# GpSimd takes low parts at the entry of an expert stage, and the unsplit half loads move from few-token to many-token steps

## The chip, the core and the metric

The kernel runs on one core of a Trainium2 chip. The metric is the device time of one execution in microseconds. Engines: TensorE (PE; its weight loads are PEld), VectorE (DVE), ScalarE (ACT), GpSimd (POOL), and SyncE (SP), which issues the loads from HBM.

## What is computed

Two layers of an encoder trunk over 256 tokens of width 1024, all in float32. The first layer ends in a dense feed-forward, the second in a mixture of eight experts, two chosen for each token. The expert part of the reference, cut to its core:

```python
logits = (t @ router)
top_v, top_i = lax.top_k(logits, 2)
top_w = jax.nn.softmax(top_v, axis=-1)
gates = sum(one_hot(top_i, 8) * top_w[..., None], axis=1)
for e in range(8):
    out = out + gates[:, e:e + 1] * ((silu(t @ w1[e]) * (t @ w3[e])) @ w2[e])
```

w1 and w3 are 1024 x 3584, w2 is 3584 x 1024. The change touches nothing ahead of this part but the routing.

## The kernel before, in words

**Split products.** A float32 product is made from faster fp32r matmuls: each operand is split into a high part (the value rounded to fp32r) and a low part (value minus high part), and three products are summed: high x high, low x high, high x low. ScalarE makes the high part of a weight (w_hi, L648), VectorE the low part (w_lo, L654). The unit of this is the half: half of a 1 MB load, 128 x 1024 elements. The program has 672 halves in the expert stage. Buffers for six split halves exist (AHEAD): ScalarE may make the high part of a half when TensorE has used the one six before.

**Experts and steps.** An expert's 3584 hidden columns are worked in 7 steps of 512, so there are 56 steps. A step has 12 halves: four of w1 (h1), four of w3 (h3), four of w2. The experts are put in an order by their number of tokens, known only at run time: positions 1, 3, 5, 7 (SMALL) have at most 64 tokens, the others at most 128. "(3,2)" is step 2 of position 3. Few-token and many-token steps alternate, after two many-token ones. TensorE's order in step i is: h1 of i, the turning of the hidden rows of step i-1 (with a fold, L1223, if that was a few-token step, or transposes, L1225), h3 of i, then w2 of step i-1. So w2 comes one step late: a few-token step's h1 and h3 are followed by the w2 of a many-token step.

**Two kinds of halves.** In a many-token step, tokens' high and low parts are two stationary operands: six matmuls of 512 columns for a half (L1154, L1155, L1158). In a few-token step the high parts of 64 tokens and their low parts share one stationary operand of 128 columns, so a half takes four (L1107, L1110), and the two sets of rows are added afterwards.

**Unsplit halves.** In some few-token steps (those of number 0, 2, 4, 6, so 16 in all) the third half of h1 isn't split: TensorE multiplies the raw float32 weights with unsplit tokens (h_few, its columns from 64 up set to zero once) in two float32 matmuls, each shown as two records (L1119). ScalarE and VectorE leave these halves out. The load's slot in the ring of ten is then free only when TensorE has used the half, while a split half frees it as soon as its low part is made.

**Order of VectorE's work in the stage.** It goes through the halves u in order; for each it does what hangs on it and then splits the half six split halves on (next_lo). At the first half of h3 of step i it makes the low part of the hidden rows of step i-1 (lower: L2211 for a many-token step, L2208 for a few-token one), which w2 of step i-1 waits for. At the second it forms other operands, at the last the product with silu (L2239). Tokens of the next expert are brought in at its eve (gather, or turn_rows at L1198), the picks of the expert after (choose, L2108) are made in step 3, its slots are told (L1213) in step 4.

**Entry.** ScalarE makes the first six high parts while VectorE computes the top two. VectorE makes the low part of half 0, then the chain of small operations: places, the picks of the first expert (choose(0)), the counts' order, most_i (the largest count, on which all engines branch between this path and a general one), then the permutation of the experts (perm_i, which SyncE reads before it can load the second expert, from the 11th load on), then the places arranged by it. After the branch it makes the low parts of the first tokens and of halves 1 to 5. TensorE gathers the first expert's tokens, with unneeded matmuls ahead (keep_busy) that keep it from falling idle. GpSimd has nothing to do there. SyncE's 11th load waits for the low parts of halves 0 and 1.

Of the kernel before, what the change touches and what calls it, by code (L numbers as in the profile page):

```python
# [14 lines left out]
P = 128  # L15
# [17 lines left out]
E = 8  # L33
# [12 lines left out]
AHEAD = 6  # L46
SMALL = (1, 3, 5, 7)
# [4 lines left out]
WHOLE_STEPS = (0, 2, 4, 6)  # L52
LAST_Q = 3
FEW_K = 2 * WHOLE_Q - 4
# [151 lines left out]
def is_few(i):  # L206
    return SEQ[i][0] in SMALL
# [7 lines left out]
class Experts:  # L215


    def __init__(self):
        self.loads = []
        for i in range(STEPS + 1):  # L220
            if i < STEPS:
                self.loads += [("h1", i, 0), ("h1", i, 1), ("h3", i, 0), ("h3", i, 1)]
            if i >= 1:
                self.loads += [("w2", i - 1, 0), ("w2", i - 1, 1)]
        self.first = {key: 2 * n for n, key in enumerate(self.loads)}
        self.halves = 2 * len(self.loads)
        self.whole = {self.first[("h1", i, 0)] + WHOLE_Q for i in range(STEPS) if is_few(i) and SEQ[i][1] in WHOLE_STEPS}
        self.split = [m for m in range(self.halves) if m not in self.whole]
        self.rank = {m: r for r, m in enumerate(self.split)}
# [7 lines left out]
def trunk_kernel(nc, x, norm1_g, w_in, w_gate, b_gate, w_branch, w_out, pool_w, pool_scale,  # L237
# [7 lines left out]
    with ExitStack() as ctx:  # L245
# [134 lines left out]
        h_few = mix(2, P)  # L380
# [59 lines left out]
        half_lo_done = sem("half_lo_done")  # L440
        half_used = sem("half_used")
# [90 lines left out]
        h_few_zero = sem("h_few_zero")  # L532
# [101 lines left out]
        def wait_half_lo(eng, m):  # L634

            eng.wait_ge(half_lo_done, m + 1)
# [14 lines left out]
        def split_half_lo(eng, m, r, halves=1):  # L651
# [4 lines left out]
                .then_inc(half_lo_done, halves)  # L656
# [94 lines left out]
        def _(pool):  # L751
# [37 lines left out]
            for l in range(L):  # L789
                pool.affine_select(out=ws[:, l, :, :], in_=ws[:, l, :, :], compare_op=ALU.is_ge, fill=0.0, base=0,  # L790
                                   pattern=[[0, 4], [-1, P]], channel_multiplier=1).then_inc(ws_lower, 1)

# [27 lines left out]
        def _(pe):  # L820
# [276 lines left out]
            keep_busy(6)  # L1097
# [30 lines left out]
            def inner_few(kind, i, toks, b, gathers=None):  # L1128
                for q in range(4):
# [3 lines left out]
                    if m in ex.whole:  # L1133
                        half_whole(m, [(h_few[:, k, :], slice(MU * k, MU * k + MU), bank[b][:, :]) for k in range(2)])
                        continue
                    outs = [(h_hi[:, 2 * q + k, toks], slice(MU * k, MU * k + MU), bank[b][:, :]) for k in range(2)]
                    half_few(m, outs, lambda x: q == 0 and x == 0, lambda x: q == LAST_Q and x == 1)
# [23 lines left out]
            def inner(kind, i, tiles, rank, gathers=None):  # L1161

                for q in range(4):
# [4 lines left out]
                    m = ex.first[(kind, i, 0)] + q  # L1168
                    half(m, rank(m), outs, lambda x: q == 0 and x % 2 == 0, lambda x: q == 3 and x % 2 == 1)
# [170 lines left out]
        def _(act_e):  # L1340
# [245 lines left out]
            def gathered_hi(e, c, b):  # L1586
                act_e.wait_ge(gathered, 2 * e + c + 1)
                n = FEW if e in SMALL else CAP
                if e in SMALL and c == 1:
                    act_e.wait_ge(h_few_zero, 1)  # L1590
                    fn(h_few[:, :, 0:FEW], bank[b][:, :].rearrange("p (k n) -> p k n", k=4)[:, FEW_K:FEW_K + 2, 0:FEW], ACT.Copy)
# [99 lines left out]
        def _(dve):  # L1691
# [438 lines left out]
            dve.tensor_reduce(most[:, :], counts[:, 0:E], AX, ALU.max)  # L2130
            step(tt(more, down(cnt), across(cnt), ALU.is_gt))
            step(dve.tensor_reduce(order, more, AX, ALU.add))
            step(ts(last_small, order, len(SMALL) - 1.0, None, ALU.is_equal))
            step(tt(last_small, last_small, counts[:, 0:E], ALU.mult))
            step(dve.tensor_reduce(third[:, :], last_small, AX, ALU.add))
            ts(most_i[:, :], third[:, :], CAP / FEW, most[:, 0:1], ALU.mult, ALU.max).then_inc(most_ready, 1)

# [31 lines left out]
            arrange(0, place, place_p)  # L2169
            dve.wait_ge(sent, 2)  # L2170
# [42 lines left out]
            def gathered_experts():  # L2213
                gathered_lo(0, 0, 5)
                split_half_lo(dve, 1, 1)
                gathered_lo(0, 1, 7)
                for m in range(2, AHEAD):
                    split_half_lo(dve, m, m)
                choose(1)
                dve.memset(h_few[:, :, FEW:P], 0.0).then_inc(h_few_zero, 1)  # L2220
# [41 lines left out]
            def all_tokens():  # L2262
# [5 lines left out]
                for m in range(1, AHEAD):  # L2268
                    split_half_lo(dve, m, m)
# [90 lines left out]
```

## Time and profile before

| | us |
|---|---|
| median of 3 runs | 1502.58 (1502.07 to 1504.14) |
| the profiled execution | 1503.12 |
| its span, first to last instruction | 1501.4 |
| TensorE busy / VectorE / ScalarE | 1452.4 / 1262.9 / 1096.6 |
| expert stage, first to last expert matmul | 626.7 to about 1491 |

The granted clock of TensorE is 0.993 of full speed over the span. From about 595 us on, the DMA engines are busy nearly without a break, at 405 to 423 GB/s in most slices. In the windows of rows 3, the stretches are the steps (1,0), (0,2), (1,1), (3,1) and (7,2). To read the rows below: times are from the span's start, and matmuls are pipelined, so a group's start to the next group's start is what it costs, not its busy time.

### The profile page before, as it was taken

The page shows a single profiled execution, that of the slowest core. Times are in us where ns is not written, and L with a number is a line of the kernel's source. Part 1 is how long each engine was busy: PE and PEld are TensorE (multiplying, and loading weights), DVE is VectorE, ACT ScalarE, POOL GpSimd, SP SyncE. Part 2 cuts the span into 40 slices and gives each one's busy share as a digit, 9 for nine tenths or more (in the row PEclk, how much of TensorE's full clock was granted, in tenths as well). Part 3 has the DMA queues.
Part 4 walks back from the last instruction along what each step waited for, and adds up shares of the span by engine and source line. Part 5 has one row for each costly group of instructions (what it writes and reads, how often), then busy time and mean ns, then how long its engine had stood idle before and what let it go on. Part 6 is the DMA issues. An engine that isn't in the chain of part 4 may idle for free.

```text
span 1501.4 us, 22229 instructions
## 1 busy us (share of the span) xinstructions
PE 1452.4 (97%) x8407; PEld 1259.6 (84%) x8407; DVE 1262.9 (84%) x1408; ACT 1096.6 (73%) x1306; POOL 94.6 (6%) x48
## 2 busy tenths in 40 slices
PE   7999989999999999999999999999999999999996
PEld 7999969999899998888877877787877887778884
DVE  5887775454588867799999999999999999999996
ACT  5685553333457663678888888888898889898885
POOL 4000000000000000000000031000040000040001
PEclk9999999999999999999999999999999999999998
DMA  9545336555444443999999999999999999999993
GB/s 278 200 148 193 141 142 222 177 188 193 144 169 173 177 158 132 408 359 421 409 421 409 409 405 416 420 421 405 412 413 423 420 409 408 421 416 421 421 421 117
DMA packets 66439, 467.02 MB, mean 311 GB/s; under 512 B 7658, under 2 KB 7894, under 8 KB 11030
## 3 DMA queue, kind: packets, MB, share of 16 engines
q1 hardware_dynamic: 63878, 458.27, 76.2%
q0 software_dynamic: 2400, 7.24, 2.4%
q8 instruction: 69, 1.13, 0.3%
q14 instruction: 44, 0.36, 0.1%
q10 hardware_dynamic: 48, 0.02, 0.0%
HBM read 460.26 MB, written 5.24 MB: 310 GB/s over the span
## 4 chain that ended last, share of the span: by engine, by line
PE 71%; DVE 19%; ACT 6%; issue 2%; DMA 1%; POOL 0%; DVEq 0%; SPq 0%; ACTq 0%
DVE w_lo L654 13%; PE bank L844 9%; PE bank L845 9%; PE bank L846 9%; PE bank L1154 9%; PE bank L1158 9%; PE bank L1155 9%; PE bank L1110 4%; PE bank L1107 4%; PE bank L1119 1%; ACT w_hi L582 1%; DMA ring<-in_w_in 1%; PE bank L1223 1%; ACT w_hi L648 1%; DVE w_lo L590 1%
## 5 line engine op out<-in xcount | busy, mean ns | idle before, releaser
L654 DVE TENSOR_TENSOR w_lo<-arena,w_hi 128x1024 fp32r<-128x1024 f32 x528 | 617.6, 1216 | 28.4 <-ACT w_hi L648 24.4
L648 ACT ACTIVATE w_hi<-arena 128x1024 fp32r<-128x1024 f32 x528 | 533.7, 1053 | 60.2 <-PE bank L1158 56.7
L590 DVE TENSOR_TENSOR w_lo<-ring,w_hi 128x2048 fp32r<-128x2048 f32 x94 | 214.9, 2289 | 128.2 <-ACT w_hi L582 127.1
L844 PE MATMUL bank<-h_hi,w_hi 128*128 128x256 f32 x992 | 283.2, 285 | 1.8 <-DVE h_lo L1748 1.7
L845 PE MATMUL bank<-h_lo,w_hi 128*128 128x256 f32 x992 | 280.6, 283 | 0.0
L846 PE MATMUL bank<-h_hi,w_lo 128*128 128x256 f32 x992 | 280.6, 283 | 0.0
L582 ACT ACTIVATE w_hi<-ring 128x2048 fp32r<-128x2048 f32 x94 | 179.7, 1913 | 105.5 <-PE bank L846 80.0
L844 PEld LDWEIGHTS bank<-h_hi,w_hi 128*128 128x128 f32 x992 | 190.2, 192 | 4.0 <-issue 2.9
L845 PEld LDWEIGHTS bank<-h_lo,w_hi 128*128 128x128 f32 x992 | 190.3, 192 | 0.5
L846 PEld LDWEIGHTS bank<-h_hi,w_lo 128*128 128x128 f32 x992 | 190.2, 192 | 0.0
L1154 PE MATMUL bank<-w_hi,h_hi 128*128 128x512 f32 x448 | 177.3, 396 | 0.0
L1155 PE MATMUL bank<-w_hi,h_lo 128*128 128x512 f32 x448 | 174.6, 390 | 0.0
L654 DVE TENSOR_TENSOR w_lo<-ring,w_hi 128x1024 fp32r<-128x1024 f32 x128 | 150.9, 1216 | 4.4 <-ACT w_hi L648 3.8
L648 ACT ACTIVATE w_hi<-ring 128x1024 fp32r<-128x1024 f32 x128 | 130.5, 1053 | 12.9 <-PE bank L1158 12.4
L1158 PE MATMUL bank<-w_lo,h_hi 128*128 128x512 f32 x448 | 138.3, 390 | 0.3 <-DVE w_lo L654 0.3
L1107 PE MATMUL bank<-w_hi,h_hi 128*128 128x512 f32 x416 | 137.5, 412 | 0.0
L1110 PE MATMUL bank<-w_lo,h_hi 128*128 128x512 f32 x416 | 128.9, 391 | 0.0
L1158 PEld LDWEIGHTS bank<-w_lo,h_hi 128*128 128x128 f32 x448 | 84.0, 188 | 18.9 <-DVE w_lo L654 0.8
L1154 PE MATMUL bank<-w_hi,act_hi 128*128 128x512 f32 x224 | 90.1, 402 | 8.8 <-DVE act_lo L2211 8.6
L1154 PEld LDWEIGHTS bank<-w_hi,h_hi 128*128 128x128 f32 x448 | 84.2, 188 | 16.8
L1155 PEld LDWEIGHTS bank<-w_hi,h_lo 128*128 128x128 f32 x448 | 84.2, 188 | 16.6
L1107 PEld LDWEIGHTS bank<-w_hi,h_hi 128*128 128x128 f32 x416 | 76.1, 188 | 20.5 <-issue 7.7
(308 smaller groups left out, 2189.9 us busy)
## 6 DMA issues: line engine op xcount, KB each, us to landing
arena<-in_moe_w SPq DMA_DIRECT2D x270, 1024.0 KB, 10.7
ring<-in_moe_w SPq DMA_DIRECT2D x66, 1024.0 KB, 10.7
ring<-in_ffn_w SPq DMA_DIRECT2D x33, 1024.0 KB, 4.8
ring<-in_w_gate SPq DMA_DIRECT2D x32, 1024.0 KB, 4.8
ring<-in_w_in SPq DMA_DIRECT2D x15, 1024.0 KB, 6.4
ring<-in_w_branch SPq DMA_DIRECT2D x8, 1024.0 KB, 4.7
ring<-in_w_out SPq DMA_DIRECT2D x8, 1024.0 KB, 4.8
x_tok<-in_x SPq DMA_DIRECT2D x2, 512.0 KB, 4.2
```

What stands on the lines that cost most here:

```text
L582: nc.scalar.activation(w_hi[:, m % HI, :], raw, ACT.Copy).then_inc(hi_ready[m % HI], 1)
L590: nc.vector.tensor_tensor(w_lo[:, m % LO, :], raw, w_hi[:, m % HI, :].bitcast(F32), ALU.subtract)\
L648: nc.scalar.activation(half_hi[:, r % AHEAD, :], raw_of(n)[:, HALF * (m % 2):HALF * (m % 2) + HALF], ACT.Copy)\
L654: eng.tensor_tensor(half_lo[:, r % AHEAD, :], raw_of(m // 2)[:, HALF * (m % 2):HALF * (m % 2) + HALF], half_hi[:, r % AHEAD, :].bitcast(F3 ...
L844: pe.matmul(out_, a[0], b[0], start=start, stop=False)
L845: pe.matmul(out_, a[0], b[1], start=False, stop=False)
L846: return pe.matmul(out_, a[1], b[0], start=False, stop=stop)
L1107: pe.matmul(dst, both, w[:, cols], start=first(x), stop=False)
L1110: last = pe.matmul(dst, both, wl[:, cols], start=False, stop=final(x))
L1154: pe.matmul(dst, hi, w[:, cols], start=first(x), stop=False)
L1155: pe.matmul(dst, lo, w[:, cols], start=False, stop=False)
L1158: last = pe.matmul(dst, hi, wl[:, cols], start=False, stop=final(x))
```

## The change

Four things are done.

1. The unsplit halves: none in few-token steps now; the third half of h1 in every many-token step but the first of all, 27 in all. The stationary operand h_whole holds all 128 tokens, and is written by ScalarE when it takes a many-token expert's tokens.
2. The low parts of halves 1, 2 and 3 are made by GpSimd, with a semaphore of their own. VectorE makes those of halves 4 and 5 after the branch.
3. VectorE computes the order and perm_i first and most_i after them; the places are arranged behind the branch, between the low parts of the tokens.
4. Four unneeded matmuls ahead of the first gather instead of six; the zeroing of h_few goes.

```diff
+POOL_LO = (1, 2, 3)
-WHOLE_STEPS = (0, 2, 4, 6)
-        self.whole = {self.first[("h1", i, 0)] + WHOLE_Q for i in range(STEPS) if is_few(i) and SEQ[i][1] in WHOLE_STEPS}
+        self.whole = {self.first[("h1", i, 0)] + WHOLE_Q for i in range(1, STEPS) if not is_few(i)}
...
         def wait_half_lo(eng, m):
-            eng.wait_ge(half_lo_done, m + 1)
+            if m in POOL_LO:
+                eng.wait_ge(pool_lo_done, POOL_LO.index(m) + 1)
+            else:
+                eng.wait_ge(half_lo_done, m + 1)
...
+            for m in POOL_LO:
+                split_half_lo(pool, m, m)
...
-            keep_busy(6)
+            keep_busy(4)
...
             def inner_few(kind, i, toks, b, gathers=None):
-                    if m in ex.whole:
-                        half_whole(m, [(h_few[:, k, :], slice(MU * k, MU * k + MU), bank[b][:, :]) for k in range(2)])
-                        continue
...
             def inner(kind, i, tiles, rank, gathers=None):
+                    if rank(m) is None:
+                        half_whole(m, [(h_whole[:, k, :], slice(MU * k, MU * k + MU), bank[tiles[0][1]][:, :]) for k in range(2)])
+                        continue
...
             def gathered_hi(e, c, b):
-                if e in SMALL and c == 1:
-                    act_e.wait_ge(h_few_zero, 1)
-                    fn(h_few[:, :, 0:FEW], bank[b][:, :].rearrange("p (k n) -> p k n", k=4)[:, FEW_K:FEW_K + 2, 0:FEW], ACT.Copy)
+                if e not in SMALL and c == 1:
+                    fn(h_whole, bank[b][:, :].rearrange("p (k n) -> p k n", k=4)[:, WHOLE_K:WHOLE_K + 2, :], ACT.Copy)
...
             step(tt(cnt, tie, counts[:, 0:E], ALU.add))
-            dve.tensor_reduce(most[:, :], counts[:, 0:E], AX, ALU.max)
             step(tt(more, down(cnt), across(cnt), ALU.is_gt))
             step(dve.tensor_reduce(order, more, AX, ALU.add))
-            step(ts(last_small, order, len(SMALL) - 1.0, None, ALU.is_equal))
-            step(tt(last_small, last_small, counts[:, 0:E], ALU.mult))
-            step(dve.tensor_reduce(third[:, :], last_small, AX, ALU.add))
-            ts(most_i[:, :], third[:, :], CAP / FEW, most[:, 0:1], ALU.mult, ALU.max).then_inc(most_ready, 1)
...
             dve.tensor_copy(perm_i[:, :], perm).then_inc(perm_ready, 1)
-            arrange(0, place, place_p)
-            dve.wait_ge(sent, 2)
+            dve.tensor_reduce(most[:, :], counts[:, 0:E], AX, ALU.max)
+            step(ts(last_small, order, len(SMALL) - 1.0, None, ALU.is_equal))
+            step(tt(last_small, last_small, counts[:, 0:E], ALU.mult))
+            step(dve.tensor_reduce(third[:, :], last_small, AX, ALU.add))
+            ts(most_i[:, :], third[:, :], CAP / FEW, most[:, 0:1], ALU.mult, ALU.max).then_inc(most_ready, 1)
...
             def gathered_experts():
                 gathered_lo(0, 0, 5)
-                split_half_lo(dve, 1, 1)
+                arrange(0, place, place_p)
                 gathered_lo(0, 1, 7)
-                for m in range(2, AHEAD):
-                    split_half_lo(dve, m, m)
+                for m in range(4, AHEAD):
+                    split_half_lo(dve, m, m, 1 if m > 4 else 1 + len(POOL_LO))
+                dve.wait_ge(sent, 2)
                 choose(1)
-                dve.memset(h_few[:, :, FEW:P], 0.0).then_inc(h_few_zero, 1)
```

## Rows read from the trace of the kernel before

**Rows 1.** The page, part 1: busy us (share of the span) xinstructions.
```profile
PE 1452.4 (97%) x8407; PEld 1259.6 (84%) x8407; DVE 1262.9 (84%) x1408; ACT 1096.6 (73%) x1306; POOL 94.6 (6%) x48
```

**Rows 2.** The page's costliest groups: busy us, mean ns, idle before.
```profile
L654 DVE TENSOR_TENSOR w_lo<-arena,w_hi 128x1024 fp32r<-128x1024 f32 x528 | 617.6, 1216 | 28.4 <-ACT w_hi L648 24.4
L648 ACT ACTIVATE w_hi<-arena 128x1024 fp32r<-128x1024 f32 x528 | 533.7, 1053 | 60.2 <-PE bank L1158 56.7
```

**Rows 3.** Windows: length; busy PE, PEld, DVE, ACT, POOL; PEclk, DMA share, GB/s.
```profile
658.90:673.15 14.25, 14.25 (x62) 11.09 (x61) 12.33 (x13) 12.53 (x15) 0.00 (x0) 1.00 0.81 329
673.15:688.60 15.45, 15.45 (x73) 12.91 (x72) 15.07 (x15) 12.99 (x15) 0.00 (x0) 1.00 1.01 424
688.60:703.20 14.60, 13.63 (x62) 10.95 (x61) 14.60 (x15) 14.26 (x17) 0.00 (x0) 1.00 1.01 418
...
905.77:920.82 15.05, 13.67 (x63) 10.95 (x61) 15.05 (x15) 14.38 (x17) 0.00 (x0) 1.00 1.02 406
...
1366.30:1380.60 14.30, 14.30 (x62) 11.11 (x62) 13.56 (x14) 12.98 (x16) 0.00 (x0) 1.00 1.01 421
```

**Rows 4.** The chain that ended last, 1340 to 1482: start, us, what.
```profile
1356.51 0.84 PE bank L1223 x8
...
1386.23 0.84 PE bank L1223 x8
...
1394.26 10.21 DVE w_lo L654 x9
1404.47 0.61 DVE act_lo L2211
...
1416.31 0.84 PE bank L1223 x8
```

**Rows 5.** Waits from 660 to 1480, SyncE's from 600: total us, times, longest.
```profile
PE bank L1154 <- DVE act_lo L2211: 8.6, 9, 1.4
...
ACT w_hi L648 <- PE bank L1158: 61.7, 201, 2.3
...
SPq L745 <- PE bank L1119: 54.7, 15, 5.1
```

**Rows 6.** Timeline of TensorE in (1,2) and (0,3): start, us, what, count.
```profile
719.64 0.62 PE L1107 MATMUL bank<-w_hi,h_hi 128*128 128x512 f32 x2
...
720.55 0.62 PE L1107 MATMUL bank<-w_hi,h_hi 128*128 128x512 f32 x2
...
724.11 0.60 PE L1225 MATMUL bank<-const,qk_raw 128*128 128x128 f32 x4
...
703.24 0.39 PE L1154 MATMUL bank<-w_hi,h_hi 128*128 128x512 f32 x1
...
704.60 0.39 PE L1154 MATMUL bank<-w_hi,h_hi 128*128 128x512 f32 x1
```

**Rows 7.** Timeline: the telling in (1,4), the picks, VectorE in (3,0).
```profile
788.38 0.50 PE L1213 MATMUL bank<-of_token,arena 128*128 128x2 f32 x4
...
722.00 0.47 DVE L2108 TENSOR_SCALAR arena<-const,place_p 128x128 f32<-128x128 f32 x2
...
878.90 2.36 DVE L654 TENSOR_TENSOR w_lo<-arena,w_hi 128x1024 fp32r<-128x1024 f32 x2 [1.99 <-ACT w_hi L648]
```

**Rows 8.** Entry: timeline, chain, one window, SyncE's issues, GpSimd's select early on.
```profile
612.94 5.77 ACT L648 ACTIVATE w_hi<-arena 128x1024 fp32r<-128x1024 f32 x6
...
626.65 0.50 PE L1154 MATMUL bank<-w_hi,h_hi 128*128 128x512 f32 x1
...
635.18 1.14 DVE w_lo L654
...
615.50:626.60 11.10, 11.06 (x56) 9.37 (x55) 8.08 (x39) 5.30 (x7) 0.00 (x0) 0.69 1.01 414
...
628.77 18.76 SPq L745 DMA_DIRECT2D arena<-in_moe_w  x8
...
L790 POOL TENSOR_SCALAR_AFFINE_SELECT arena<-arena 128x512 f32<-128x512 f32 x2 | 3.8, 1927 | 8.2 <-DMA arena<-in_sgu_w 8.2
```

More of the change, by code:

```diff
@@ L51 @@
 WHOLE_Q = 2
-WHOLE_STEPS = (0, 2, 4, 6)
-LAST_Q = 3
-FEW_K = 2 * WHOLE_Q - 4
+WHOLE_K = 2 * WHOLE_Q - 4
 MORE = 8
@@ L379, in trunk_kernel @@
         picks = mix(2, TT, CAP)
-        h_few = mix(2, P)
+        h_whole = mix(2, P)
         half_hi = w_hi[:, :, :].rearrange("p a (b c) -> p (a b) c", c=HALF)
@@ L440, in trunk_kernel @@
         half_lo_done = sem("half_lo_done")
+        pool_lo_done = sem("pool_lo_done")
         half_used = sem("half_used")
@@ L531, in trunk_kernel @@
         eye_set = sem("eye_set")
-        h_few_zero = sem("h_few_zero")
         gate_ready = sem("gate_ready")
@@ L655, in split_half_lo @@
                               half_hi[:, r % AHEAD, :].bitcast(F32), ALU.subtract)\
-                .then_inc(half_lo_done, halves)
+                .then_inc(pool_lo_done if m in POOL_LO else half_lo_done, halves)
         def drams(key):
@@ L1132, in inner_few @@
                     m = ex.first[(kind, i, 0)] + q
-                    if m in ex.whole:
-                        half_whole(m, [(h_few[:, k, :], slice(MU * k, MU * k + MU), bank[b][:, :]) for k in range(2)])
-                        continue
                     outs = [(h_hi[:, 2 * q + k, toks], slice(MU * k, MU * k + MU), bank[b][:, :]) for k in range(2)]
-                    half_few(m, outs, lambda x: q == 0 and x == 0, lambda x: q == LAST_Q and x == 1)
+                    half_few(m, outs, lambda x: q == 0 and x == 0, lambda x: q == 3 and x == 1)
                     if kind == "h3" and q == 0:
@@ L2267, in all_tokens @@
                         .then_inc(all_lo, 1)
-                for m in range(1, AHEAD):
-                    split_half_lo(dve, m, m)
+                for m in range(4, AHEAD):
+                    split_half_lo(dve, m, m, 1 if m > 4 else 1 + len(POOL_LO))
+                arrange(0, place, place_p)
+                dve.wait_ge(sent, 2)
                 weights()
```

## Prediction

> **What bounds the kernel now.** I read the page first. TensorE is busy for 1452 us of the span and VectorE for 1263 us [rows 1], so the shares alone say that TensorE is the limit, with VectorE next. The change works almost wholly in the expert stage, from about 626 us to 1490 us. I read that stage from three views.
>
> First the engine times of single steps [rows 3], each from its first h1 matmul to the next step's. A many-token step takes 15.45 us and TensorE is busy for all of it, while VectorE is busy for 15.07. A few-token step with an unsplit half takes 14.30 us, all of it TensorE, with VectorE at 13.56. A few-token step without one takes 14.60 us, but there VectorE is busy for all of it and TensorE for only 13.63. So the bound alternates: TensorE in many-token steps, VectorE in few-token steps that have all their halves split.
>
> Then the chain of waits [rows 4], whose fold of hidden rows (L1223, once in each many-token step) marks pairs of steps. The pair from 1356.51 to 1386.23 has an unsplit half and takes 29.72 us. The pair from 1386.23 to 1416.31 has none and takes 30.08 us; its chain passes through act_lo at L2211. The pair with more TensorE work is the shorter one.
>
> Last the waits [rows 5]: in the expert stage TensorE waits for L2211 and ScalarE for TensorE; no compute engine waits for a transfer there. Why L2211 is late in a few-token step: twelve "fast" halves lie in a row (w2 of the step before last, then h1 and h3 of this one), each 0.91 us on TensorE against 1.13 us on VectorE (1.216 us long, but nine in 10.21 us as they overlap) [rows 2, 4, 6]. VectorE works at most six halves ahead, and L2211 waits in its order behind the splits. In the "slow" stretch (w2 of a many-token step, h1, h3, at 1.36 us a half [rows 6]) VectorE catches up, and idles: 0.38 us of step 673.15 to 688.60 [rows 3].
>
> **The change part by part.** The profiled execution took 1503.12 us (span 1501.4); the median of the runs shown is 1502.58, 0.5 us less. Sums are made against 1503.12.
>
> *Price of an unsplit half on TensorE.* In few-token step (1,2) the four halves of h1 run from 719.64 to 724.11, 4.47 us; the first takes 0.91 (719.64 to 720.55). So the unsplit one costs 4.47 - 3 x 0.91 = 1.74 us, its slow successor included [rows 6]. In a few-token step it replaced four matmuls: +0.83. In a many-token step it replaces six, 1.36 us (703.24 to 704.60): +0.38, and I use 0.37 from the mean of all.
>
> *A. 27 unsplit halves added in many-token steps (steps 1 to 55).* TensorE bounds these steps, and their VectorE and ScalarE have idle time already. The unsplit half lies at h1, the third of its step. The split it spares VectorE falls six halves earlier, in the slow stretch, where VectorE catches up anyway; five split halves more follow before the fast stretch, so VectorE enters that with the same full lead as before. Nothing is given back: 27 x 0.37 = **+10.0 us**.
>
> *B. 16 unsplit halves taken out of few-token steps.* TensorE does 0.83 us less, VectorE one split more (1.13), in the middle of the fast stretch. The step turns into the VectorE-bound kind that the trace shows: the pair goes from 29.72 to 30.08, +0.36 [rows 4]. So taken for the five later steps with nothing else in them ((1,6), (3,6), (5,6), (7,2), (7,4)): +1.8. In (1,4), (3,4), (5,4) the matmuls that tell the slots (0.50 us long, some 0.36 of it by itself, L1213) lie ahead of w2 and hide that much [rows 7]: 0. In (1,2), (3,2), (5,2) VectorE also makes the picks (0.47 us, 0.4 with the overlap, L2108 [rows 7]): about +0.75 each; in the first of them two tellings give TensorE 0.9 us of other work, so only +0.15: together +1.65. Sum **+3.4**.
>
> *C. First steps of the few-token experts.* In (3,0) ScalarE first empties the results and VectorE then stands idle for 1.99 us waiting for it [rows 7]; one more high part there (1.05 us, [rows 2]) goes straight in front of ScalarE's next work, which TensorE's join waits for: +1.0, three times ((3,0), (5,0), (7,0)). In (1,0) VectorE is busy for only 12.33 of 14.25 us [rows 3], so it loses 0.83 and gets back some 0.3 of stall: -0.5. Sum **+2.5**.
>
> *D. Second steps (3,1), (5,1), (7,1).* VectorE comes into them behind, from the step before; the unsplit half in the many-token step between lets it catch up. They fall from the 15.05 us that (3,1) takes [rows 3] to the 14.60 of (1,1): three times 0.4, **-1.2**.
>
> *E. Entry.* GpSimd takes the low parts of halves 1 to 3, that is 3 x 1.13 = 3.4 us from VectorE; the rearranging of the places (0.6 us) moves behind the branch. The six high parts are made from 612.94 to 618.7, one each 0.96 us, and TensorE starts half 0 at 626.65 [rows 8], so it wants the low part of half 1 at about 628 and of half 3 at 631. GpSimd's speed is not in the trace: at VectorE's pace 1.2 us a half, by its nearest row (a select over 128x512, 1.93 us [rows 8]) 3.9 us, which ends the third at about 615 + 11.6 = 626.6. Both are in time, so the speed costs nothing. The only stall that VectorE's backlog makes here is at the low part made from 635.18 to 636.32, 0.6 us on TensorE (half 6 takes 1.97 us in place of 1.36) [rows 8]: gone. most_i comes some 0.9 us later (behind the four steps of the order), and TensorE's first expert matmul follows ScalarE's and VectorE's branch: the gather's end is no longer what counts, so two keep-busy matmuls less buy nothing: 626.65 to about 626.9, +0.2. The order's earlier end lets SyncE issue the eleventh load about 4 us sooner (628.77 before); behind it wait all later loads, and no engine waits for loads. Sum -0.4, and +0.3 for port sharing (below): **-0.1**. The Trainium skill ("GPSIMD Engine Reference", 3.1 Elementwise) puts a two-input operation of 2048 columns at 4497 ns on GpSimd and 2293 on VectorE; the trace's 1216 ns for 1024 columns on VectorE fits that [rows 2], GpSimd's isn't shown. By it, an estimate from that page, a half takes 2.4 us and the sum stays as it is.
>
> *F. End.* Step (7,6) is the last, and behind it only the last splits are made, ScalarE's and then VectorE's. It loses its unsplit half: -0.83 if TensorE set the end, +1.13 if the last low part does [rows 2]. The trace's chain ends on ScalarE and VectorE there, with some idle time ahead of them: **+0.4**.
>
> Total 10.0 + 3.4 + 2.5 - 1.2 - 0.1 + 0.4 = +15.0, or 1518.1 against the profiled run, 1517.6 as a median.
>
> **The rivals.**
> *R1, faster: the spared splits are shared.* 27 instead of 16 halves unsplit takes 11 x 1.13 = 12.4 us off VectorE. If VectorE's lead at the start of the fast stretch grew with the many-token step's unsplit half, the few-token steps would lose their stall as well. Then TensorE's sum decides: +10.0 - 16 x 0.83 - 0.7 = -4.0, **1498.6**. For it: VectorE is full in those steps. Against: it idles just before them, so its lead is capped by buffers, not by work. It decides if no TensorE wait for L2211 is left in a common few-token step; from an average stall of 0.5 instead of 1.2 us in 28 steps the time is still near 1507.
> *R2, slower still: GpSimd disturbs the routing at the entry.* Its operations run from 615 to 619 at the least and 626.6 at the most, beside VectorE's chain of small ones, which is on the path: VectorE is busy for 8.08 us from 615.50 to 626.60 [rows 8], of which 1.22 and 0.69 are larger ones with slack. If the 6.2 left took twice as long, the time would be 1517.6 + 6.2 - 0.3 = **1523.5**. The trace has no such overlap; the chain's operations are tiny, which speaks against the full price, so I carry 0.3. The Trainium skill says in the same page (1. Specifications) that GpSimd shares its SBUF interfaces with VectorE instructions that have two SBUF inputs; most of the chain's have. That speaks for this rival.
> *R3: the ring of loads.* SyncE can refill a slot whose half is unsplit only when TensorE has used it; such waits are 54.7 us in 15 now [rows 5] and become 27. In 658.90 to 673.15 the DMA share fell to 0.81; in 1366.30 to 1380.60, also with such a wait, it stayed 1.01 [rows 3]: the queue is deep enough later. If it drained each time, 0.2 x 14 = 2.8 us of transfer would be lost in each pair, and beyond a few pairs the loads would set the pace: about **1530** at 10 pairs. Slower steps make it less likely.
> *R4: the change doesn't do what it says.* A stall partly relieved and an unsplit half somewhat dearer behind other matmuls: within 1509 to 1513.
>
> **How the numbers follow.** Forecast 0.77, **1517.6** (own range 1513 to 1522, from B between 0 and +6 and the entry); R1 0.08; R2 0.08; R3 0.02; R4 0.05. The range 1509 to 1523.5 leaves out R1, R3 and the far end of R2. A measurement tells 0.2% (3 us) from no change: faster is 0.07, same 0.04 (the space between R1 and R4), slower 0.89.
>
> **What would show it.** A: each many-token step 15.8 instead of 15.45 us with TensorE busy throughout, and 108 fp32 matmul records instead of 64. B: pairs of about 30.45 us, act_lo (L2211 of before) on the chain in nearly every one, and TensorE's wait for it up from 8.6 us in 9 to some 20 in 25. C, D: (3,0) at 17.1, (3,1) at 14.6. E: the wait at 635 gone, the eleventh load issued near 624.5. The forecast is wrong if few-token steps come out at 13.5 us (R1), if the stretch from 615 to 627 grows by over a microsecond (R2), or if ScalarE or TensorE waits for a load (R3).

## Result and the profile after

The changed kernel's median is 1527.05 us (1523.68 to 1529.20, five runs), against 1502.58 before (1502.07 to 1504.14, also five). The ratio is 1.0163, 95% interval 1.0148 to 1.0178: slower by 24.5 us. The forecast was 1517.6 with a range to 1523.5: the direction was right, the size 9.4 us short and outside the range. The profiled execution took 1524.43 us (span 1522.7), 21.3 more than the profiled one of before.

The page's busy line and its two costliest groups, which answer [rows 1, 2]:

```profile
PE 1453.9 (95%) x8351; PEld 1251.2 (82%) x8351; DVE 1250.7 (82%) x1393; ACT 1083.4 (71%) x1295; POOL 99.7 (7%) x51
...
L656 DVE TENSOR_TENSOR w_lo<-arena,w_hi 128x1024 fp32r<-128x1024 f32 x515 | 600.8, 1216 | 49.9 <-ACT w_hi L650 46.7
L650 ACT ACTIVATE w_hi<-arena 128x1024 fp32r<-128x1024 f32 x518 | 522.7, 1053 | 55.8 <-PE bank L1160 52.4
```

VectorE has 12 us less work and TensorE 1.5 more, and the kernel is 21 longer: nearly all of it went into waits of TensorE. The windows of the steps (1,0), (0,2), (1,1), (3,0), (3,1) and (7,2), with the columns of [rows 3]:

```profile
665.51:679.07 13.56, 13.56 (x63) 11.01 (x62) 13.40 (x14) 13.40 (x16) 0.00 (x0) 1.00 0.98 360
679.07:694.89 15.82, 15.82 (x72) 12.55 (x71) 14.01 (x14) 11.92 (x14) 0.00 (x0) 1.00 0.94 388
694.89:709.53 14.64, 13.67 (x63) 10.95 (x62) 14.64 (x15) 14.13 (x17) 0.00 (x0) 1.00 1.00 412
883.69:900.58 16.89, 14.27 (x63) 10.86 (x62) 14.67 (x15) 16.77 (x21) 3.24 (x1) 1.00 0.99 400
916.40:931.03 14.63, 13.71 (x63) 10.95 (x62) 14.63 (x15) 14.12 (x17) 0.00 (x0) 1.00 1.01 425
1385.26:1399.89 14.63, 13.66 (x63) 10.95 (x62) 14.63 (x15) 14.12 (x17) 0.00 (x0) 1.00 1.01 422
```

Many-token step (0,2) is 0.37 longer, with TensorE busy throughout. Few-token step (7,2) now has VectorE busy throughout and TensorE idle for 1 us. The chain that ended last reads the same way in the other pairs from 1350 us on (here 1375 to 1406, start to start 30.45 us against 29.72 in [rows 4]), and TensorE's wait for act_lo has doubled against [rows 5]:

```profile
1375.30 0.84 PE bank L1228 x8
...
1383.32 10.21 DVE w_lo L656 x9
1393.53 0.61 DVE act_lo L2212
...
1405.75 0.84 PE bank L1228 x8
```

```profile
PE bank L1156 <- DVE act_lo L2212: 18.3, 20, 1.4
```

So far the forecast holds. It fails at the entry. VectorE's timeline there, then GpSimd's three operations (shortest, median, longest in ns, first and last start), then TensorE's timeline:

```profile
616.77 0.17 DVE L2083 TENSOR_TENSOR eq<-bank,top 128x16 f32<-128x16 f32 x1
616.98 1.96 DVE L2084 TENSOR_TENSOR eq<-eq,rank 128x16 f32<-128x16 f32 x1
618.97 0.17 DVE L2085 TENSOR_REDUCE best<-eq 128x2 f32<-128x16 f32 x1
619.18 2.07 DVE L2086 TENSOR_TENSOR hot<-rank,best 128x16 f32<-128x16 f32 x1
621.28 0.17 DVE L2091 SCALAR_TENSOR_TENSOR lg<-hot,bank 128x16 f32<-128x16 f32 x1
...
621.69 1.85 DVE L2083 TENSOR_TENSOR eq<-lg,top 128x16 f32<-128x16 f32 x1
```

```profile
L656 POOL TENSOR_TENSOR w_lo<-arena,w_hi x3: 2332/2337/2910, 616.0 to 621.2; 128x1024 fp32r<-128x1024 f32 x3
```

```profile
624.43 0.59 PE L1096 MATMUL bank<-chosen,ones 128*128 128x8 f32 x2 [6.11 <-DVE chosen L2094]
...
628.43 5.43 PE L1193 MATMUL bank<-arena,shared8k 128*128 128x128 f32 x32
633.62 0.48 PE L1156 MATMUL bank<-w_hi,h_hi 128*128 128x512 f32 x1
```

Three operations over 16 columns, 0.17 us each before, take 1.96, 2.07 and 1.85. Each ends as one of GpSimd's does (at 618.9, 621.2 and 623.5). Those between them with a bank of PSUM or nothing beside their one SBUF input (L2083's first, L2085, L2091) keep 0.17. That is 5.37 us more on the chain that TensorE waits for.

The profiled 21.3 us are then:

- 0.99 already there when the routing starts (616.57 against 615.58), most of it from a stretch at half clock (1.2 instead of 2.4 GHz) at 219 us, in a part that the change doesn't touch;
- 5.98 from there to the first expert matmul;
- -0.68 in step (0,0);
- +14.33 in steps 1 to 54;
- +0.70 from (7,6) to the end.

Of the 5.98, 5.37 are the three operations. The gather's matmuls (L1193) take 5.19 instead of 3.71, at a granted clock of 0.66 instead of 0.96, and the two keep-busy matmuls fewer give back 0.86. The gather's 1.48 can't be put down to GpSimd: in e4 and e8 below, where GpSimd does nothing at the entry, the same matmuls take 5.47 and 5.05.

### The profile page after: what moved, and what is told of

It reads as the page before. It is cut to its first block, busy times and chain, and to the rows that moved or that the text cites. A ratio compares the mean times of both kernels' runs of the same rounds, so it can differ in the third digit from the quotient of the medians.

```text
span 1522.7 us, 22090 instructions
## 1 busy us (share of the span) xinstructions
PE 1453.9 (95%) x8351; PEld 1251.2 (82%) x8351; DVE 1250.7 (82%) x1393; ACT 1083.4 (71%) x1295; POOL 99.7 (7%) x51
## 4 chain that ended last, share of the span: by engine, by line
PE 66%; DVE 23%; ACT 7%; issue 2%; DMA 1%; POOL 0%; SPq 0%; ACTq 0%; DVEq 0%
DVE w_lo L656 16%; PE bank L1156 10%; PE bank L849 9%; PE bank L1157 9%; PE bank L1160 9%; PE bank L850 9%; PE bank L851 9%; PE bank L1124 3%; ACT w_hi L650 2%; PE bank L1228 2%; ACT w_hi L581 1%; DMA ring<-in_w_in 1%; DVE w_lo L589 1%; DVE act_lo L2212 1%; DVE qk_raw L2240 1%
## 5 line engine op out<-in xcount | busy, mean ns | idle before, releaser
L656 DVE TENSOR_TENSOR w_lo<-arena,w_hi 128x1024 fp32r<-128x1024 f32 x515 | 600.8, 1216 | 49.9 <-ACT w_hi L650 46.7
L650 ACT ACTIVATE w_hi<-arena 128x1024 fp32r<-128x1024 f32 x518 | 522.7, 1053 | 55.8 <-PE bank L1160 52.4
L1156 PE MATMUL bank<-w_hi,h_hi 128*128 128x512 f32 x394 | 167.2, 424 | 0.0
L1157 PE MATMUL bank<-w_hi,h_lo 128*128 128x512 f32 x394 | 154.0, 391 | 0.0
L1112 PE MATMUL bank<-w_hi,h_hi 128*128 128x512 f32 x448 | 141.0, 396 | 2.0 <-DVE h_hi L2189 2.0
L1115 PE MATMUL bank<-w_lo,h_hi 128*128 128x512 f32 x448 | 138.6, 391 | 0.0
L1160 PE MATMUL bank<-w_lo,h_hi 128*128 128x512 f32 x394 | 121.8, 390 | 0.0
L1156 PE MATMUL bank<-w_hi,act_hi 128*128 128x512 f32 x224 | 91.1, 407 | 18.5 <-DVE act_lo L2212 18.3
L1112 PEld LDWEIGHTS bank<-w_hi,h_hi 128*128 128x128 f32 x448 | 81.9, 188 | 17.6 <-DVE h_hi L2189 3.2
L1157 PEld LDWEIGHTS bank<-w_hi,h_lo 128*128 128x128 f32 x394 | 74.2, 188 | 20.0 <-issue 6.4
L1156 PEld LDWEIGHTS bank<-w_hi,h_hi 128*128 128x128 f32 x394 | 74.1, 188 | 20.0 <-issue 6.5
```

The lines of the kernel that those rows point to most:

```text
L650: nc.scalar.activation(half_hi[:, r % AHEAD, :], raw_of(n)[:, HALF * (m % 2):HALF * (m % 2) + HALF], ACT.Copy)\
L656: eng.tensor_tensor(half_lo[:, r % AHEAD, :], raw_of(m // 2)[:, HALF * (m % 2):HALF * (m % 2) + HALF], half_hi[:, r % AHEAD, :].bitcast(F3 ...
L1112: pe.matmul(dst, both, w[:, cols], start=first(x), stop=False)
L1115: last = pe.matmul(dst, both, wl[:, cols], start=False, stop=final(x))
L1156: pe.matmul(dst, hi, w[:, cols], start=first(x), stop=False)
L1157: pe.matmul(dst, lo, w[:, cols], start=False, stop=False)
```

## Experiments

Three theories stood at the start. L: GpSimd's subtractions hold those VectorE operations that read two SBUF inputs, each until GpSimd's instruction has ended. K: the delay comes from the entry's other edits, the later release of the gather and the fewer matmuls. M, on the sizes: the entry holds less than its 7 us of the median, and the steps hold more, through stretches at half clock. The "before" of each group of runs is measured beside it: 1502.42, 1503.28, 1502.96 and 1503.51 us.

**The change taken apart.** `e1_no_gpsimd` is the changed kernel without GpSimd's part:

```diff
-POOL_LO = (1, 2, 3)
+POOL_LO = ()
...
                 gathered_lo(0, 0, 5)
+                split_half_lo(dve, 1, 1)
                 arrange(0, place, place_p)
...
-                for m in range(4, AHEAD):
+                for m in range(2, AHEAD):
```

> The changed kernel with the three low parts given back to VectorE; the new order at the entry, the four matmuls that keep the engine busy and the moved unsplit halves stay. Theory L (GpSimd's subtractions hold VectorE's small two-input operations until each ends): the operations at L2083, L2084 and L2086 are back near 0.17 us, the first expert matmul is back near 626.7, and only the unsplit move's +14.5 is left: 1517 us (1516 to 1519). Rival K (the delay comes from the later release of the gather and the two fewer matmuls): the first expert matmul stays near 633 and the time near 1524 to 1527.

`e2_unsplit_only` is the kernel before with only this, and the matching copy into h_whole:

```diff
-        self.whole = {... for i in range(STEPS) if is_few(i) and SEQ[i][1] in WHOLE_STEPS}
+        self.whole = {... for i in range(1, STEPS) if not is_few(i)}
```

> The kernel before with the unsplit halves moved to the many-token steps, its entry untouched. The sum of the prediction for the steps (A to D) is +14.7, and the changed kernel's steps read +14.3: 1517 us (1516 to 1518.5), the pair of steps 30.45. Theory M (of the 24.5 us at the median the entry holds less than its 7 us, and the steps more through stretches at half clock that the unsplit halves bring): 1519.5 or more, with the granted clock below 0.990.

`e3_entry_only` is the other half of the diff alone, `e4_reorder_only` the same without GpSimd's part:

> The kernel before with everything that the change does at the entry (GpSimd's low parts, the order computed sooner, four matmuls instead of six), its unsplit halves untouched. Theory L: the profile shows the 7 us at the first expert matmul, less about 0.5 in the first step, 1509.5; with all of the median's surplus over the profiled run put at the entry, 1512. Theory M: 1508 or less. The prediction's own term E would give 1502.5.

> The kernel before with the order computed sooner, the arrangement behind the first gathered low part and four matmuls instead of six, without GpSimd's low parts. Theory L: the gather starts 0.2 to 0.3 us later and the stall of 0.6 us behind it stays or goes: 1502.4 to 1503.2, not told from before. Rival K: the first expert matmul is 5 us or more later, 1507 to 1510.

The last column is from each profiled execution: from the first operation of the routing to the first expert matmul.

| kernel | median us | ratio to before, 95% | routing to first expert matmul, us |
|---|---|---|---|
| before | 1502.42 | | 11.07 |
| e1 no GpSimd | 1519.41 | 1.0108 (1.0085 to 1.0131) | 10.70 |
| e2 unsplit move only | 1523.10 | 1.0135 (1.0104 to 1.0167) | 10.68 |
| e3 entry only | 1507.71 | 1.0033 (1.0022 to 1.0044) | 16.87 |
| e4 entry without GpSimd | 1504.50 | 1.0006 (0.9993 to 1.0019) | 11.98 |

K falls: the reordering and the fewer matmuls alone can't be told from no change. With GpSimd's part the same three operations take 1.96, 2.07 and 1.85 us again, to the hundredth, and without it 0.17 or 0.18. The first expert matmul of e1 comes at 629.45, not near 626.7 as expected, since its routing starts at 618.75, 3.2 us later than before's, behind stretches at half clock earlier on; so the last column is the one to compare. It is 16.87 to 17.05 in the three kernels whose GpSimd subtracts whole halves beside the routing (the changed one, e3, e15) and 10.68 to 12.41 in those where GpSimd does nothing until the order is known.

But e2 is 6 us above the prediction's sum, on theory M's side, and above e1, which has more in it (the intervals overlap); e3 too is where M has it. The steps of e2 say why. (3,0), (5,0) and (7,0) take 18.11 to 18.13 us, not 16.89 to 16.91 as in the changed kernel's profile, and (3,5) takes 18.38, not 16.78. The window of (3,0) in e2 (granted clock 0.91) and TensorE's timeline in it:

```profile
876.04:894.15 18.11, 15.56 (x63) 12.09 (x62) 15.90 (x16) 17.09 (x22) 4.61 (x1) 0.91 0.99 394
```

```profile
880.70 0.70 PE L1104 MATMUL bank<-w_hi,h_hi 128*128 128x512 f32 x2
...
883.76 0.69 PE L1122 MATMUL bank<-act_lo,eye_r 128*128 128x512 f32 x1 [1.90 <-ACT act_lo L1609]
884.25 1.05 PE L1104 MATMUL bank<-w_hi,h_hi 128*128 128x512 f32 x2
```

TensorE waits 1.90 us for ScalarE, and after that its matmul pairs take 1.05 us instead of 0.62: the clock is at 1.2 GHz for 3.4 us. The changed kernel has the same wait of 1.90 us at 891.55, without the slow stretch in that execution. In the kernel before, the wait at this matmul of (3,0) is 0.20, and the longest wait of that step 0.78, at another place:

```profile
881.45 0.50 PE L1125 MATMUL bank<-act_lo,eye_r 128*128 128x512 f32 x1 [0.20 <-ACT act_lo L1613]
```

That gave a new theory, W: a wait this long is followed by a stretch at half clock in some executions and not in others, and the move makes three such waits, in (3,0), (5,0) and (7,0).

**What holds VectorE.** `e5_gpsimd_copies` has the whole entry edit, but GpSimd copies the three halves (pool.tensor_copy from the raw half) and VectorE makes the low parts over the copy. In its expectation L1 and L2 are theories, not lines:

> The kernel before with the whole entry of the change, but GpSimd only copies the three halves (one input instead of two) where it subtracted, at the same time; VectorE then makes the low parts itself. Theory L2 (only a GpSimd instruction with two inputs holds VectorE's small operations with two SBUF inputs): they take 0.17 us and the set of chosen experts is ready near 617.9 on the span's clock. Theory L1 (any long GpSimd instruction does): two or three operations take 1 to 2 us, and it is ready 3 us or more later. The low parts that VectorE then makes again cost nothing that shows: 1502 to 1505 by L2, 1505 to 1509 by L1.

`e6_pieces`:

```diff
-                split_half_lo(pool, m, m)
+                for a in range(0, HALF, 256):
+                    last = pool.tensor_tensor(half_lo[:, m, a:a + 256], raw_of(m // 2)[:, ...], half_hi[:, m, a:a + 256].bitcast(F32), ALU.subtract)
+                last.then_inc(pool_lo_done, 1)
```

> The kernel before with the whole entry of the change, each of GpSimd's three subtractions cut into four of 256 columns, the same work in twelve instructions. Theory L (a VectorE operation with two SBUF inputs waits until the GpSimd instruction that runs has ended, and then goes ahead of the next): the held operations are more in number but wait 0.3 to 0.7 us each instead of 1.9, and the chosen experts are ready 3 to 5 us later than before, as they can meet up to twelve instructions, none longer than 0.7 us. Rival S (shared bandwidth: they are slowed by a factor while GpSimd reads): the same three operations or so take the same 1.9 us, since their own size and GpSimd's traffic are unchanged. Rival Q (VectorE waits until GpSimd's queue is empty): one operation takes 5 us or more.

VectorE and GpSimd in e5, then in e6:

```profile
621.05 0.60 DVE L2086 TENSOR_TENSOR eq<-eq,rank 128x16 f32<-128x16 f32 x1
...
621.89 0.74 DVE L2088 TENSOR_TENSOR hot<-rank,best 128x16 f32<-128x16 f32 x1
...
623.08 0.54 DVE L2085 TENSOR_TENSOR eq<-lg,top 128x16 f32<-128x16 f32 x1
...
620.05 3.54 POOL L797 CAST w_lo<-arena 128x1024 fp32r<-128x1024 f32 x3 [581.77 <-ACT w_hi L650]
...
L797 POOL CAST w_lo<-arena x3: 1028/1035/1574, 620.0 to 622.6; 128x1024 fp32r<-128x1024 f32 x3
```

```profile
623.22 0.17 DVE L2095 TENSOR_REDUCE best<-eq 128x2 f32<-128x16 f32 x1
623.42 0.45 DVE L2096 TENSOR_TENSOR hot<-rank,best 128x16 f32<-128x16 f32 x1
623.90 0.65 DVE L2104 TENSOR_TENSOR chosen<-hot 128x16 f32<-128x16 f32 x1
...
625.83 0.79 DVE L2108 TENSOR_SCALAR place_p<-chosen 128x16 f32<-128x16 f32 x1
626.65 1.70 DVE L659 TENSOR_TENSOR w_lo<-arena,w_hi 128x1024 fp32r<-128x1024 f32 x1
...
619.81 9.80 POOL L803 TENSOR_TENSOR w_lo<-arena,w_hi 128x256 fp32r<-128x256 f32 x12 [583.92 <-ACT w_hi L653]
...
L803 POOL TENSOR_TENSOR w_lo<-arena,w_hi x12: 717/724/1702, 619.8 to 628.9; 128x256 fp32r<-128x256 f32 x12
```

A copy with one input holds them too, so L2 falls, though L1 had the size wrong: they take 0.54 to 0.74 us, not 1 to 2, and the chosen experts are ready 1.4 us later, not 3. What counts is how long GpSimd's instruction still runs: a copy takes 1.03 us (the first 1.57), a piece 0.72, a whole subtraction 2.33 (the first 2.91). In e6 no small operation is held longer than one piece, so S (slowed by a factor, whatever GpSimd's instruction) and Q (until its queue is empty) fall as well.

| GpSimd at the entry | routing to chosen experts, us | routing to first expert matmul, us |
|---|---|---|
| none (before; e4) | 2.44; 2.45 | 11.07; 11.98 |
| three copies (e5) | 3.81 | 11.98 |
| twelve pieces (e6) | 4.16 | 15.18 |
| three whole subtractions (e3) | 7.81 | 16.87 |

The pieces hold more operations, nine ahead of VectorE's first split, and keep GpSimd busy for longer (9.80 instead of 7.51 us), but each hold is short: the experts are chosen 1.7 us late instead of 5.4, where the expectation had 3 to 5. In this one execution the pieces cost less than whole subtractions. The times of e5 and e6 (1507.42 and 1510.74 us, one run each) can't be compared with the others: their routing starts at 620.64 and 620.39, 5 us later than before's, which was so before GpSimd began.

By these rows the holding goes both ways. The first instruction of GpSimd starts in each case while VectorE's last operation ahead of the routing (shared8k<-x_tok,rstd,prod) still runs, and takes 0.5 to 0.6 us more than the next; and the piece of 1.70 us in e6 starts at 627.23, while VectorE's split runs from 626.65 to 628.35. In e6 a TENSOR_SCALAR with one SBUF input is held too (0.79); the reduction never is. The Trainium skill ("SBUF — State Buffer", Who interferes with whom) says that VectorE and GpSimd share one pair of ports under an exclusive lock for the whole instruction, that a VectorE operation with two SBUF inputs contends with a GpSimd one that reads SBUF, tensor_scalar can, and a reduction doesn't. All four agree with these rows; a small TENSOR_SCALAR (most_i, 128x1) beside a running subtraction in e9 and e14 kept its 0.21 us.

**The same work at another moment.** `e9_gpsimd_late` is e3 and `e14_late_in_after` the changed kernel, each with one line more:

```diff
+            pool.wait_ge(perm_ready, 1)
             for m in POOL_LO:
                 split_half_lo(pool, m, m)
```

> The kernel before with the whole entry of the change, but GpSimd begins its three low parts only when the order is known, behind the small operations. Theory L: the small operations take 0.17 us again, the gather starts within 0.3 us of before, and the held operations are the arrangement and the low parts of the gathered tokens: the second half's low part is there 3 us after the order, about when TensorE wants it, and the third and fourth 2.5 and 5 us later, each about 1 us late: 1503 to 1505.5. Rival (the delay belongs to the entry's other edits): 1507.5 as with everything at the entry.

> The changed kernel with one wait more: GpSimd begins its three low parts only when the order is known. Nothing else differs. Theory L: the three held operations are back at 0.17 us and with them 5.5 us at the first expert matmul: 1519.5 to 1521.5. If part of the entry's loss belonged to the moved release of the gather or the fewer matmuls, it stays: 1523 or more.

e9: 1502.82 us, ratio 0.9998 (0.9986 to 1.0010). e14: 1520.48 us, ratio 1.0108 (1.0091 to 1.0125), 6.6 below the changed kernel. From the routing to the first expert matmul they take 11.86 and 12.06 us. In e14 GpSimd starts at 623.35 and the small operations are at 0.17 again:

```profile
615.85 0.17 DVE L2085 TENSOR_TENSOR eq<-eq,rank 128x16 f32<-128x16 f32 x1
...
616.26 0.18 DVE L2087 TENSOR_TENSOR hot<-rank,best 128x16 f32<-128x16 f32 x1
...
623.35 7.08 POOL L656 TENSOR_TENSOR w_lo<-arena,w_hi 128x1024 fp32r<-128x1024 f32 x3 [585.17 <-DVE perm_i L2167]
```

In e9 GpSimd holds only the arrangement (1.29 instead of 0.28 us) and two splits, which nothing waits for. There step (0,0) is 10.98 us against 11.67, so GpSimd's low parts do buy what the prediction said, 0.6 us, when they lie behind the chain; the median of e9 can't show a gain this small.

**Terms A to D by themselves.** `e12_both` has the unsplit halves in the many-token steps and its own 16; `e8_few_none` has none anywhere (WHOLE_STEPS = ()); `e7_few_all_whole` has WHOLE_STEPS = (0, 1, 2, 3, 4, 5, 6).

> The kernel before with unsplit halves in the many-token steps in addition to its own 16; entry untouched. It is term A by itself. By the prediction the many-token steps grow by 0.37 each, 27 times, 10.0 us, since TensorE sets them; what VectorE is spared shows only in (1,1), (3,1), (5,1), (7,1) and (7,3), 0.4 each, 2 us at most: 1510.5 to 1512.5. Rival R1 (what is spared is shared, and A is smaller): 1507 or less.

> The kernel before with no unsplit half in any step; entry untouched. It is terms B, C and D by themselves. By the prediction's separate terms the few-token steps come to +4.7 and the many-token ones stay at 15.45: 1507 to 1508.5. Rival (the lead of VectorE's splits over TensorE is carried from step to step, and the unsplit halves of the many-token steps refill it in the changed kernel): more than +6, with few-token steps over 14.63, 1510 or more.

> The kernel before with an unsplit half in all 28 few-token steps instead of 16, many-token steps and entry untouched. Term B read backwards: where a few-token step without one is longer than 14.25 us, VectorE's splits set it, and one split less brings it there: (1,1) 14.63, (3,1), (5,1) and (7,1) 15.05, (3,4) and (5,4) 14.74 and (1,4) fall by 0.4 to 0.8 each, the steps without an idle TensorE stay: 4 to 6 us less, 1496.5 to 1499. Rival R1 of the prediction in reverse (what is spared is shared, or the lead of the splits is what counts): within 1 us of before.

The windows of (3,1) and (7,2) in e12, of (3,0) and (3,1) in e8, of (3,1) in e7:

```profile
912.11:926.76 14.65, 13.72 (x63) 10.97 (x62) 14.65 (x15) 14.04 (x17) 0.00 (x0) 1.00 1.01 426
1378.48:1392.74 14.26, 14.26 (x63) 11.10 (x62) 13.54 (x14) 12.94 (x16) 0.00 (x0) 1.00 1.01 422
```

```profile
877.29:894.33 17.04, 14.28 (x63) 10.85 (x62) 14.78 (x15) 16.92 (x21) 3.20 (x1) 1.00 1.00 405
909.79:924.84 15.05, 13.69 (x63) 10.95 (x62) 15.05 (x15) 14.26 (x17) 0.00 (x0) 1.00 1.02 406
```

```profile
908.33:922.59 14.26, 14.26 (x63) 11.10 (x62) 13.95 (x14) 12.94 (x16) 0.00 (x0) 1.00 1.02 405
```

- e12: 1513.06 us, ratio 1.0068 (1.0044 to 1.0092). Its many-token steps read +9.86 together, (3,1), (5,1), (7,1) -1.28, every other few-token step within 0.05 but for the half-clock stretches in (1,5) and (5,5). R1 falls: the unsplit halves there are paid in full and give back D alone.
- e8: 1514.54 us, ratio 1.0075 (1.0050 to 1.0099), 6 us above its expectation. Without half-clock stretches its steps read +6.0: B and C, forecast 5.9 together, while D is absent, (3,1) being still at 15.05, since it needs the many-token halves. That is 1.3 of the 6; it also has the long waits in (3,0), (5,0) and (7,0) of theory W, and how the rest divides isn't known.
- e7: 1499.38 us, ratio 0.9972 (0.9960 to 0.9984), faster than before: (1,1), (3,1), (5,1), (7,1), (7,3) and (7,5) fall to TensorE's 14.26, and (3,5) and (5,5) by 0.46. (1,4), (3,4) and (5,4) stay at 14.74, against the expectation. Without half-clock stretches the steps sum to -5.0, and from (7,6) to the end it is 0.7 longer.

**The new waits and the clock.** `e11_first_kept` is e2, `e15_first_kept_after` the changed kernel, each with the unsplit halves of (1,0), (3,0), (5,0), (7,0) kept:

```diff
+WHOLE_STEPS = (0,)
...
-        self.whole = {... for i in range(1, STEPS) if not is_few(i)}
+        self.whole = {... for i in range(1, STEPS) if not is_few(i) or SEQ[i][1] in WHOLE_STEPS}
```

> The kernel before with the unsplit halves in the many-token steps, and of those in few-token steps only the four of the steps (1,0), (3,0), (5,0) and (7,0) kept; entry untouched. Theory C (the first few-token step of a pass is the one that a further split reaches): (3,0), (5,0) and (7,0) are back at 16.1 from 16.9, (1,0) goes back to 14.25 and the wait of 1.9 us in the middle of those steps to 0.8, so 1.7 us less than with the unsplit move alone. Theory W (a wait of TensorE of 1.9 us or more is what a stretch at half clock follows, and the move makes three more such waits, in just these steps): 1.2 us more for each stretch that is gone, in all 3 to 5 us less than 1523.1, 1518 to 1520. Without W: 1521 to 1522, and stretches at half clock still in or behind these steps.

> The changed kernel, entry and all, with the unsplit halves of (1,0), (3,0), (5,0) and (7,0) kept beside those of the many-token steps, so that TensorE's wait in the middle of (3,0), (5,0) and (7,0) is 0.8 us instead of 1.9. By the steps' lengths alone (three times -0.8, +0.7 in (1,0)) 1525.3. Theory W (each such wait is followed by a stretch at half clock in some executions, 1.2 us each): another 1 to 3.5 us less, 1521.5 to 1524.5, and the granted clock nearer 0.991 than 0.987 in most runs.

e11: 1515.31 us, ratio 1.0086 (1.0053 to 1.0120), 7.8 below e2. e15: 1520.66 us, ratio 1.0120 (1.0103 to 1.0137), 6.4 below the changed kernel. Both came out below what W expected: the steps' lengths give 1.7 and three stretches at 1.22 another 3.7 at most, and the rest isn't explained. In e11 the wait at the join of (3,0) is 0.19 us again and the longest of the step 0.77, and in e14, which keeps the waits of 1.89, (3,0) has the half-clock stretch and (7,0) has not, within one execution. Windows of (3,0) in e11, and of (3,0) and (7,0) in e14:

```profile
877.31:893.39 16.08, 15.07 (x62) 10.87 (x61) 13.63 (x14) 15.96 (x20) 3.27 (x1) 1.00 0.96 393
```

```profile
877.74:895.84 18.10, 15.56 (x62) 12.08 (x61) 15.89 (x16) 17.13 (x21) 4.54 (x1) 0.91 0.98 396
1321.74:1338.62 16.88, 14.28 (x62) 10.86 (x61) 14.66 (x15) 16.76 (x21) 3.30 (x1) 1.00 0.98 381
```

The same can be counted over steps 1 to 54 of all 16 profiled executions here, with the longest wait of TensorE in each step:

| longest wait in the step, us | steps | with a stretch at half clock |
|---|---|---|
| up to 1.4 | 807 | 0 |
| 1.87 to 1.96, in (3,0), (5,0), (7,0) | 15 | 5 |
| 2.21, in (1,5), (3,5), (5,5) | 42 | 17 |

The waits of 2.21 us are in the kernel before too, and in all others but e7 and e13. There the unsplit half of these steps brings them down to 0.96, and none of the six has such a stretch. The 22 stretches begin between 0.2 us before the end of the wait and 1.5 us after it. From the kernel before, then from e7, the same matmul of (1,5):

```profile
820.58 0.66 PE L1198 MATMUL bank<-const,shared8k 128*128 128x128 f32 x4 [2.21 <-DVE h_lo L2190]
...
824.71 0.66 PE L1198 MATMUL bank<-const,shared8k 128*128 128x128 f32 x4 [0.96 <-DVE h_lo L2190]
```

Over the span, the changed kernel's granted clock was 0.991 and 0.990 in its two shortest runs and 0.987, 0.987, 0.986 in the longer ones (1527.05 to 1529.20 us). e15's was 0.991 to 0.993 in all, with times within 2.8 us. The unprofiled executions of the changed kernel were not seen by step, so where their surplus of 2.6 us lies is inferred from e2, e14 and e15: stretches in (3,0), (5,0) and (7,0), but (3,5) and (5,5), where the profiled execution had none either, can hold part of it.

**Both gains together.** `e13_best` is e7 with e9's entry:

> The kernel before with an unsplit half in all 28 few-token steps and, at the entry, the order computed sooner and GpSimd's three low parts started behind the order. The two parts lie in different stages and add: 3.9 us less from the steps and 0.5 less from the first step: 1498 to 1499.5, against 1502.9. If the entry's part was only chance: 1499.4 as with the steps alone.

1498.40 us, ratio 0.9965 (0.9952 to 0.9979): the fastest kernel here, though not told from e7 alone.

## Why the prediction was right and wrong

- *What bounds the steps:* right. TensorE sets the many-token steps and VectorE the few-token ones with all halves split. The steps 1 to 54 sum to +14.33, forecast 14.7. The 108 records of unsplit matmuls, the pairs of 30.45 us and (3,1) at 14.63 came as said, and TensorE's wait for act_lo is 18.3 us in 20 for some 20 in 25.
- *A, +10.0:* 9.8 measured, 9.86 by itself in e12. R1 failed for the reason given: what VectorE is spared falls where it catches up anyway.
- *B, +3.4:* 4.15. Its (1,2), (3,2) and (5,2) are +2.07 rather than 1.65, and (1,6), (3,6), (5,6), (7,2), (7,4) +2.1 rather than 1.8; (1,4), (3,4), (5,4) +0.0.
- *C, +2.5:* 1.70, with +0.8 instead of 1.0 for (3,0), (5,0), (7,0) and -0.69 in (1,0). The mechanism, ScalarE ahead of TensorE's join, was right. But the term had only a length. It turned a wait of 0.20 us at the join into one of 1.90, and the step said nothing of the clock, though the trace of before has (1,5) with a wait of 2.21 us at 18.37 us and (3,5) and (5,5) with the same wait at 16.78. Each such stretch cost 1.2 us in (3,0), (5,0) and (7,0); they are a likely part of the 2.6 us between the changed kernel's median and its profiled run.
- *D, -1.2:* -1.30.
- *F, +0.4:* +0.70 in this pair of executions, but little of it is the unsplit half. From the start of (7,6) to the last group of w2 matmuls the kernels that lose it and have no stretch at half clock there (e11, e14, e15) take 16.85 or 16.86 us, against 16.72 to 16.74 in before, e3, e4, e5 and e6: +0.1. The rest is a stretch at half clock behind a wait of 2.00 us in (7,6), and the part behind it, which takes 13.7 to 14.6 us from one kernel's execution to the next's. That 0.70 is near 0.4 is luck.
- *E, -0.1:* this is the step that failed: +5.3 in the profiled run (5.98 at the first expert matmul, -0.68 in the first step). The stall of 0.6 us did go. The clause "+0.3 for port sharing" was the mis-sized term: 5.37. The mechanism was named as R2, with a chance of 0.08, and priced by a factor of two over the whole chain. That its 6.2 us lies near 5.37 is luck: most of the chain kept its 0.17 us, and three operations took over ten times theirs. The operations' small size was taken as speaking against it. It speaks the other way: an operation that is held waits for the end of GpSimd's instruction, whatever its own size, so three instructions of 2.5 us on a chain that is almost all such operations can cost up to their whole time, 7.5 us (an estimate; 5.37 was measured). And "both are in time, so the speed costs nothing" looked only at who waits for the result; it is GpSimd's speed that sets the length of each hold. The 2.4 us a half, the estimate by the Trainium skill ("GPSIMD Engine Reference", 3.1 Elementwise), was near the 2.33 to 2.91 measured. The gather's end, which "is no longer what counts", was what the first expert matmul followed here, without idle time between.
- *The eleventh load:* forecast near 624.5, it came at 630.81, since the order itself was late (perm_i at 629.58 instead of 624.02).
- *R3:* fell. SyncE's waits for unsplit halves are 27 now, 107.7 us together, and still no compute engine waits for a load in the expert stage.

The miss of 9.4 us at the median is, in profiled terms, E (5.3 instead of -0.1) and 0.99 from before the routing, less 0.4 in the steps and plus 0.3 at the end, 6.3; the other 3.1 is how the medians lie to the profiled runs: 2.6 above it now, 0.5 below it before.

## What to carry to other kernels

- Work handed to GpSimd is costed twice: when its result is due, and which VectorE operations with two SBUF inputs lie beside it. Each of those can lose the rest of a GpSimd instruction. Where they must overlap, shorter GpSimd instructions hold each one for less. Start GpSimd behind a latency chain of VectorE, not beside it.
- Take relief from the engine that sets the step in question. The unsplit half pays in steps that VectorE sets (e7, -3.9 us) and costs in those that TensorE sets (+0.37 each), whatever the totals of the engines say.
- A wait of TensorE that grows from 0.2 to 1.9 us can cost its own length and a stretch at half clock behind it; list the long waits of a stage before and after.
- Compare a piece of a kernel from an event in front of it, not from the start of the span: the routing of these kernels starts anywhere from 614.5 to 620.9 us, by stretches at half clock in a part that is the same in all.

## What the runs showed of the hardware

- GpSimd on 128x1024 fp32: 2.33 us to subtract, against VectorE's 1.22, but 1.03 to copy; 0.72 for a subtraction of 256 columns. Instructions that ran into one of VectorE's took 2.91, 1.57 and 1.25 to 1.70 instead.
- A held VectorE operation shows in the trace as a long operation (1.96 us for 16 columns), not as idle time before it, and the same three values come back in e3.
- Waits of 1.9 to 2.2 us of TensorE were followed by 3.4 us at 1.2 GHz in 22 of 57 cases, at 1.2 to 1.6 us each; none of the 807 steps with shorter waits, of steps 1 to 54 in 16 executions, had such a stretch. How one execution differs from the next isn't settled.
